# Half-size transfers for the weight chunks of two feed-forward blocks, and another order of PSUM pairs for their last downward product

## The chip, the cores and the metric

The program runs on one core of a Trainium2 chip. The metric is the device time of one execution in microseconds (us), here the median of the runs shown. The engines are TensorE (PE, matrix products; PEld is its loading of weights), VectorE (DVE), ScalarE (ACT), GpSimd (POOL) and SyncE (SP, which here only asks for transfers).

## What is computed

A decoder layer on 1024 tokens of width 1024: a SwiGLU block, a block of three attention branches, a second SwiGLU block. The change touches only the two SwiGLU blocks (d_ff is 2816, 22 tiles of 128):

```python
def _swiglu(h, w_gu, w_down):
    a, b = jnp.split(h @ w_gu, 2, axis=-1)
    return (jax.nn.silu(a) * b) @ w_down

x = x + 0.5 * _swiglu(_rmsnorm(x, ffn1_norm[l]), ffn1_w_gu[l], ffn1_w_down[l])
...
x = x + 0.5 * _swiglu(_rmsnorm(x, ffn2_norm[l]), ffn2_w_gu[l], ffn2_w_down[l])
```

All is float32. The kernel gets that accuracy from a faster format: every operand is split into a high part (`_hi`) and the rest (`_lo`), and each product is three matmuls, hi by hi, hi by lo and lo by hi.

## The kernel before, in words

The instruction streams of the engines are written out by hand, one function per engine; each engine works through its own stream in order, and semaphores tie the streams together. So an instruction that waits holds up all that stands behind it on its engine.

**The feed-forward part.** `ffn(f)` is run twice, f = 0 and f = 1. Its first four tiles are done plainly. The other 18 (`t` = 4 to 21) and the nine pairs of tiles on the way down (`kind` "pair") are done with seven products in place of eight (Strassen's scheme), so sums of blocks of weights are needed. The list `PARTS` is the order: an even tile alone (seven parts), then an odd tile and a pair, whose parts alternate. Two tiles and a pair, 21 parts, are called a triple here; each part is 12 matmuls of 128x512 on PE, so a triple has 252. There are nine triples in each pass. The first pair comes in the first triple, behind the first part of tile 5. Behind the last triple stands the last way down (`kind` "down", four parts, the eight output tiles m = 0 to 7, `down_part`, L2298).

**The weights.** `CHUNK` lists what is loaded: one chunk of 1 MB for each tile and each pair and one for the last way down, 28 in a pass. They alternate between two places, `raw2[0]` and `raw2[1]`, each of two halves of 512 KB. SP asks for chunk c when the last part of chunk c-2 has been split (`chunks`, L718; semaphore `part_split`, counted by DVE). For a pair, c-2 is the even tile of its triple: the pair's chunk is asked for when that tile's last part has been split, and the pair's first part is two places further on in `PARTS`.

**One part's way through the engines.** POOL forms the sums that the part needs (`weights_sum`, L768: S1 and S2, where S2 overwrites one block of the chunk, then S3 and S4). ACT copies to `q_hi` (`part_hi`, L947), DVE subtracts to `q_lo` (`part_lo`, L1526) and counts `part_split`. `q_hi`, `q_lo` and `q_sum` are a ring of four, so a place comes free when PE has done the part four back. For the first part of a pair both S1 and S2 must be there before ACT can copy. DVE works two parts ahead of PE in its stream (`part_lo(f, n + 2)` in `ffn`). Between them stand its other jobs: additions of PSUM results to tiles, the low parts of activations, and `pair_add` (L1523), which adds what a pair's part left in PSUM to `xT`.

**PSUM** is four pairs of banks, `ps[:, 0]` to `ps[:, 3]`. A tile's parts use banks 0 to 3 (pairs 0 and 1); a pair's part uses `ps[:, 2]` for its first six matmuls and `ps[:, 3]` for the others; the last way down also uses `ps[:, 2 + m % 2]`. PE begins a part of a pair, and each output tile m of the last way down, when DVE has taken out what was in that pair of banks (`down_added`).

**Behind the last way down.** In pass 0 DVE and ACT make the operands of the next stage from `xT` while PE works on: `h_hi` (ACT), `h_lo` (DVE, L1387), squares (ACT) summed by POOL (`acc`, then `acc_lo`, L768). PE takes them up in `streamed` and `norm_sum`. In pass 1 PE transposes each finished tile of `xT` (`y_turn`, L2836, into `ps[:, m % 2]`), ACT copies it out and SP stores it.

Of the kernel before, what the change touches and what calls it, by code (L numbers as in the profile page):

```python
# [25 lines left out]
P = 128  # L26
# [122 lines left out]

def add_begin(g):  # L150

    return DT + EVENTS * (g - 1) if g else 0


def chunk_end(c):

    return max(n for n, part in enumerate(PARTS) if part[3] == c) + 1
BR = (HS * HD + 2 * HD + HX * HD) // P
# [164 lines left out]
def layer(nc, x, mem, weights, gains, head_gains, rel_bias, consts, onehot, out):  # L323
    ctx = ExitStack()
    with ctx:
# [172 lines left out]
        raw_in = [sem(f"raw_in{i}") for i in range(NRAW)]  # L498
        hi_done, split_done, unit_done = sem("hi_done"), sem("split_done"), sem("unit_done")
# [201 lines left out]
        def _(sp):  # L701
# [32 lines left out]
            for k in range(U_SB, U_SB + NRAW):  # L734
                if k % NRAW == (CHUNKS - 1) % NRAW:
                    sp.wait_ge(part_split, chunk_end(CHUNKS - NRAW) + 1)
                else:
                    sp.wait_ge(part_split, chunk_end(CHUNKS - NRAW))
                load(k)
# [16 lines left out]
        def _(pool):  # L756
# [13 lines left out]
            def weights_sum(f, n, i, name):  # L770
# [3 lines left out]
                if kind == "tile":  # L774
                    a11, a12, a21, a22 = (raw2[c % 2][:, r, cols] for r in range(2) for cols in BOTH)
# [90 lines left out]
        def _(act):  # L866
# [80 lines left out]
            def part_hi(f, n):  # L947
# [3 lines left out]
                after_chunk(act, f, c)  # L951
# [21 lines left out]
                elif p == 2:  # L973
                    act.wait_ge(w_summed, W_SUMS * f + sums_through(n))
                    src = raw2[c % 2][:, 1, T0]
                else:
                    src = raw2[c % 2][:, p // 6, 512 * (p > 0):512 * (p > 0) + 512]
# [394 lines left out]
        def _(dve):  # L1372
# [79 lines left out]
            def add_tile(f, g, m):  # L1452
# [11 lines left out]
                nc.vector.tensor_tensor(xT[:, m, :], xT[:, m, :], ps[:, 2 + m % 2, :], ALU.add).then_inc(down_added, 1)  # L1464
# [60 lines left out]
            def part_lo(f, n):  # L1525
# [27 lines left out]
                elif p == 2:  # L1553
                    src = raw2[c % 2][:, 1, T0]
                else:
                    src = raw2[c % 2][:, p // 6, 512 * (p > 0):512 * (p > 0) + 512]
# [570 lines left out]
        def _(pe):  # L2127
# [115 lines left out]
            def down_mm(m, q, hi, lo, t, first, final, halves=BOTH, within=None):  # L2243

                for cols in halves:
                    if within and cols == T1:
                        within()
                    mm(ps[:, 2 + m % 2, cols], hi, a_hi[t % 4][:, cols], first, False)
                    mm(ps[:, 2 + m % 2, cols], hi, a_lo[t % 4][:, cols], False, False)
                for cols in halves:  # L2250
                    last = mm(ps[:, 2 + m % 2, cols], lo, a_hi[t % 4][:, cols], False, final)
                return last

            def down_plain(f):
# [3 lines left out]
                def whole(m, q):  # L2258
                    return down_mm(m, q, w_hi[:, w_slot(u + 1 + q), m, :], w_lo[:, w_slot(u + 1 + q), m, :], q, q == 0, q == 1)
# [38 lines left out]
            def down_part(f, n, finish):  # L2298
# [4 lines left out]
                def whole(m, q, halves=BOTH, within=None):  # L2303
                    at_ = P * (2 * q + m % 2)
                    return down_mm(m, q, q_hi[n % NQ][:, at_:at_ + P], q_lo[n % NQ][:, at_:at_ + P], 2 * g + q, q == 0, q == 1,
                                   halves, within)
# [75 lines left out]
            def proj(n, hi, lo, there=None, k0=0, k1=DT):  # L2382
# [20 lines left out]
                if n == PR_SB:  # L2403
# [544 lines left out]
```

## Time and profile before

| | us |
|---|---|
| median of 3 runs | 2198.47 |
| lowest and highest | 2197.08, 2198.56 |
| the profiled execution, its own time | 2196.08 |
| its span in the profile | 2194.2 |
| mean granted TensorE clock, of full speed | 0.998 |

PE is busy in 98% of the span. The page of the profile gives busy times, the chain of work that ended last and the costliest groups. For a change of this kind the timeline (instructions in order of time), the waits and the windows (busy time and granted clock in a chosen stretch) are read too. In a row of the timeline the first number is the start, the second the duration, both in us; a bracket at its end gives how long the engine was idle just before, and what it then waited for. Durations of matmuls overlap: two of them in a row start closer together than one lasts.

### The profile page before, as it was taken

What the parts mean: (1) busy time and instruction counts of PE and PEld (TensorE: products, weight loads), DVE (VectorE), ACT (ScalarE), POOL (GpSimd) and SP (SyncE); (2) the same over time, 40 slices, a digit from 0 to 9 for tenths busy, and PEclk for the clock granted to TensorE, in tenths of its full rate; (3) what the DMA queues carried; (4) which work ended last, traced back from release to release, by engine and by line L of the source; (5) the groups of instructions that cost most, each with busy time, mean ns of one, the idle gap of its engine ahead of it and who ended that gap; (6) DMA issues with size and microseconds to landing.
All of it is one profiled execution on the core that took longest, in us unless ns stands there. A gap on an engine that the chain in (4) does not pass through costs nothing.

```text
span 2194.2 us, 26286 instructions
## 1 busy us (share of the span) xinstructions
PE 2160.8 (98%) x9968; PEld 1733.5 (79%) x9968; DVE 1578.4 (72%) x1809; ACT 908.6 (41%) x1433; POOL 453.1 (21%) x396
## 2 busy tenths in 40 slices
PE   8999999999999999999999999999999999999998
PEld 7787888888887777777778888888887888888887
DVE  7878888888888688877535343354877888888885
ACT  6333333333335677846442111233233333344332
POOL 3013322223323122221000000012013322233320
PEclk9999999999999999999999999999999999999999
DMA  5111111111112300011112111131111111111113
GB/s 172 62 50 57 58 58 58 49 35 52 58 58 84 115 20 29 20 48 39 39 21 77 48 58 48 48 125 39 49 49 57 58 58 58 43 37 57 58 58 96
DMA packets 46733, 126.54 MB, mean 58 GB/s; under 512 B 3405, under 2 KB 20077, under 8 KB 46352
## 3 DMA queue, kind: packets, MB, share of 16 engines
q1 hardware_dynamic: 44704, 112.60, 15.5%
q10 hardware_dynamic: 912, 10.11, 1.2%
q0 software_dynamic: 992, 2.15, 0.5%
q8 instruction: 80, 1.31, 0.2%
q14 instruction: 45, 0.37, 0.0%
HBM read 116.42 MB, written 9.87 MB: 58 GB/s over the span
## 4 chain that ended last, share of the span: by engine, by line
PE 78%; DVE 9%; DMA 5%; POOL 4%; issue 3%; ACT 1%; POOLq 0%; DVEq 0%; SPq 0%; ACTq 0%
PE ps L2129 76%; DMA raw<-in_weights 4%; POOL raw L789 2%; POOL q_sum L786 2%; DVE h_lo L1387 1%; DVE q_lo L1557 1%; DVE xT L1523 1%; DVE q_lo L1546 1%; DVE b_sum_lo L1510 1%; DVE a_full L1590 1%; POOL q_sum L792 1%; DVE tok_lo L1439 1%; PE ps L2744 0%; DVE xT L1731 0%; PE ps L2679 0%
## 5 line engine op out<-in xcount | busy, mean ns | idle before, releaser
L2129 PE MATMUL ps<-tok_hi,q_hi 128*128 128x512 f32 x1008 | 392.5, 389 | 0.0
L2129 PE MATMUL ps<-tok_lo,q_hi 128*128 128x512 f32 x1008 | 392.1, 389 | 0.0
L2129 PE MATMUL ps<-tok_hi,q_lo 128*128 128x512 f32 x1008 | 392.1, 389 | 0.0
L2129 PE MATMUL ps<-h_hi,w_hi 128*128 128x512 f32 x960 | 373.1, 399 | 1.7 <-ACT h_hi L1112 1.1
L2129 PE MATMUL ps<-h_lo,w_hi 128*128 128x512 f32 x960 | 363.9, 391 | 0.7 <-DVE h_lo L2041 0.6
L1523 DVE TENSOR_TENSOR xT<-xT,ps 128x1024 f32<-128x1024 f32 x252 | 302.1, 1216 | 33.8 <-PE ps L2129 23.1
L2129 PE MATMUL ps<-h_hi,w_lo 128*128 128x512 f32 x960 | 305.5, 391 | 0.0
L2129 PEld LDWEIGHTS ps<-tok_hi,q_hi 128*128 128x128 f32 x1008 | 189.2, 188 | 40.2 <-issue 1.1
L2129 PEld LDWEIGHTS ps<-h_hi,w_hi 128*128 128x128 f32 x960 | 179.9, 188 | 51.3 <-issue 15.7
L2129 PEld LDWEIGHTS ps<-tok_hi,q_lo 128*128 128x128 f32 x1008 | 189.2, 188 | 39.4
L2129 PEld LDWEIGHTS ps<-tok_lo,q_hi 128*128 128x128 f32 x1008 | 189.2, 188 | 39.1
L2129 PE MATMUL ps<-b_hi,q_hi 128*128 128x512 f32 x504 | 200.9, 399 | 11.0 <-DVE q_lo L1546 5.9
L2129 PEld LDWEIGHTS ps<-h_hi,w_lo 128*128 128x128 f32 x960 | 180.2, 188 | 38.9 <-DVE w_lo L1380 0.5
L2129 PEld LDWEIGHTS ps<-h_lo,w_hi 128*128 128x128 f32 x960 | 180.1, 188 | 36.2 <-DVE h_lo L2041 1.7
L786 POOL TENSOR_TENSOR q_sum<-raw 128x512 f32<-128x512 f32 x72 | 73.1, 1015 | 608.2 <-DMA raw<-in_weights 419.7
L2129 PE MATMUL ps<-b_hi,q_lo 128*128 128x512 f32 x504 | 197.6, 392 | 0.0
L1380 DVE TENSOR_TENSOR w_lo<-raw,w_hi 128x1024 fp32r<-128x1024 f32 x84 | 115.1, 1372 | 76.8 <-ACT w_hi L878 67.4
L2129 PE MATMUL ps<-a_lo,q_hi 128*128 128x512 f32 x352 | 138.6, 394 | 0.0
L765 POOL TENSOR_TENSOR acc<-acc,sq 128x1024 f32<-128x1024 f32 x21 | 53.9, 2564 | 408.0 <-ACT sq L885 407.9
L2129 PEld LDWEIGHTS ps<-b_hi,q_hi 128*128 128x128 f32 x504 | 95.4, 189 | 43.7 <-DVE q_lo L1546 14.3
L1557 DVE TENSOR_TENSOR q_lo<-raw,q_hi 128x512 fp32r<-128x512 f32 x144 | 112.2, 779 | 21.3 <-ACT q_hi L978 21.3
L1981 DVE TENSOR_TENSOR gate<-ps,rB 128x1024 f32<-128x1024 f32 x24 | 29.4, 1224 | 129.9 <-PE ps L2129 129.9
(309 smaller groups left out, 3682.0 us busy)
## 6 DMA issues: line engine op xcount, KB each, us to landing
raw<-in_weights SPq DMA_DIRECT2D x56, 1024.0 KB, 5.0
raw<-in_weights SPq DMA_DIRECT2D x83, 512.0 KB, 3.5
x_keep<-xT ACTq DMA_DIRECT2D x1, 4096.0 KB, 12.4
x_back<-x_keep ACTq DMA_DIRECT2D x1, 4096.0 KB, 12.1
x_nat<-in_x SPq DMA_DIRECT2D x7, 512.0 KB, 7.4
out<-y_nat SPq DMA_DIRECT2D x7, 512.0 KB, 3.2
toe_keep<-toe_row ACTq DMA_DIRECT2D x2, 704.0 KB, 5.8
m_nat<-in_mem SPq DMA_DIRECT2D x1, 1024.0 KB, 8.0
```

Of the source, the lines that this page charges most:

```text
L765: nc.gpsimd.tensor_tensor(acc[:], acc[:], sq[:, k % 2, :], ALU.add).then_inc(acc_done, 1)
L786: nc.gpsimd.tensor_tensor(to, a21, a22, ALU.add).then_inc(w_summed, 1)
L789: nc.gpsimd.tensor_tensor(a21, to, a11, ALU.subtract).then_inc(w_summed, 1)
L792: nc.gpsimd.tensor_tensor(to, a12, a21, ALU.subtract).then_inc(w_summed, 1)
L1380: nc.vector.tensor_tensor(w_lo[:, w_slot(k)].rearrange("p a b -> p (a b)"), raw[:, k % NRAW, :], w_hi[:, w_slot(k)].rearrange("p a b -> p ...
L1387: nc.vector.scalar_tensor_tensor(out=h_lo[:, k, :], in0=xT[:, k, :], scalar=g32[:, gain, k:k + 1], in1=h_hi[:, k, :].bitcast(F32), op0=ALU ...
L1439: nc.vector.tensor_tensor(tok_lo[i][:], tok[i][:], tok_hi[i][:].bitcast(F32), ALU.subtract).then_inc(tok_split, 1)
L1510: nc.vector.tensor_tensor(b_lo(g, i), b_full(g, i), b_hi[i][:].bitcast(F32), ALU.subtract).then_inc(a_ready, 1)
L1523: nc.vector.tensor_tensor(to, to, ps[:, 2 + half, :].rearrange("p (a c) -> p a c", a=2), ALU.add).then_inc(down_added, 1)
L1557: nc.vector.tensor_tensor(q_lo[n % NQ][:], src, hi, ALU.subtract).then_inc(part_split, 1)
L1981: nc.vector.tensor_tensor(gate_tile(m, b), ps[:, merge_pair(m, b), :], rB[:], ALU.mult).then_inc(mg_taken, 1)
L2129: return pe.matmul(o, a, b, start=start, stop=stop, skip_group_check=True)
```

## The change

Three things are done.

1. Each chunk is brought in by two transfers of 512 KB. Each is asked for when its own half of the place is free (`half_end`): for a tile behind parts 4 and 6, for a pair behind parts 3 and 6, for the last way down behind parts 1 and 3. The tile's weights are laid out anew on the host, so that a half is what parts 0 to 4, or 5 and 6, read (S1 of a tile still reads both). POOL and ACT wait for the half or halves that a part reads; the odd places get semaphores of their own (`chunk_in`).
2. The last way down uses other pairs of PSUM: in pass 0 pairs 1, 0, 2, 3, 1, 0, 2, 3 for m = 0 to 7, in pass 1 pairs 1, 0 and then 2, 3 in turn (`end_pair`). m = 0 and 1 so wait for the last tile's readers (`seven_added`, `glu_done`) and not for the last pair's additions. PE's next users of pair 0 wait for the additions (`PR_SB`, `y_turn`).
3. In pass 1 the transposes move to later places: none behind m = 1, two behind m = 5.

```diff
+def end_pair(f, m):
+
+    return (1, 0, 2, 3)[m % 4] if f == 0 or m < 2 else 2 + m % 2
...
+def half_end(c, half):
+
+    kind, of = CHUNK[c]
+    return part_at(kind, of, {"tile": (4, 6), "pair": (3, 6), "down": (1, 3)}[kind][half]) + 1
...
-        def after_chunk(eng, f, c):
-
-            eng.wait_ge(raw_in[c % 2], 16 * ((U_HALVES[f] + 6) // 2 + CHUNKS // 2 * f + c // 2 + 1))
+        def after_chunk(eng, f, c, *halves):
+
+            for half in halves:
+                if c % 2:
+                    eng.wait_ge(chunk_in[half], 16 * (CHUNKS // 2 * f + c // 2 + 1))
+                else:
+                    eng.wait_ge(raw_in[half], 16 * ((U_HALVES[f] + 6) // 2 + CHUNKS // 2 * f + c // 2 + 1))
...
-                    if c == 0:
-                        sp.wait_ge(split_done, U_HALVES[f] + 6)
-                    elif c == 1:
-                        sp.wait_ge(unit_done, U_HALVES[f] + 6)
-                    else:
-                        sp.wait_ge(part_split, NPART * f + chunk_end(c - 2))
-                    sp.dma_start(raw2[c % 2][:], weights[chunk_at(f, c):chunk_at(f, c) + 2].rearrange("a p n -> p a n")
-                                 ).then_inc(raw_in[c % 2], 16)
+                    for half in range(2):
+                        if c == 0:
+                            sp.wait_ge(split_done, U_HALVES[f] + 6)
+                        elif c == 1:
+                            sp.wait_ge(unit_done, U_HALVES[f] + 6)
+                        else:
+                            sp.wait_ge(part_split, NPART * f + half_end(c - 2, half))
+                        sp.dma_start(raw2[c % 2][:, half, :], weights[chunk_at(f, c) + half]
+                                     ).then_inc((raw_in, chunk_in)[c % 2][half], 16)
...
                 if i == 0:
                     after_slot(pool, f, n)
-                    after_chunk(pool, f, c)
+                    after_chunk(pool, f, c, *((0, 1) if kind == "tile" else (0,) if p < 4 else (1,)))
...
-                after_chunk(act, f, c)
+                if kind == "tile":
+                    after_chunk(act, f, c, 0 if p < 5 else 1)
+                elif kind == "pair":
+                    after_chunk(act, f, c, *((0,) if p < 3 else (0, 1) if p == 3 else (1,)))
+                else:
+                    after_chunk(act, f, c, p // 2)
...
-                    for m in range(2):
-                        pe.wait_ge(down_added, G + m - 1)
-                        whole(m, 0)
+                    pe.wait_ge(seven_added, 3 * TILES7 * (f + 1))
+                    whole(0, 0)
+                    pe.wait_ge(glu_done, (TILE_COUNT - 2) * (f + 1))
+                    whole(1, 0)
                 pe.wait_ge(a_ready, A_COUNT * (f + 1))
                 for m in (2 * p, 2 * p + 1):
                     if p:
-                        pe.wait_ge(down_added, G + m - 1)
+                        pe.wait_ge(down_added, G + m - (1 if f or p == 1 else 3))
...
                 if n == PR_SB:
+                    pe.wait_ge(down_added, ADD_COUNT - 2)
...
+                if m == 0:
+                    pe.wait_ge(down_added, 2 * ADD_COUNT - DT + 2)
...
-            ffn(1, lambda m: y_turn(m - 1) if m else None)
+            def y_behind(m):
+
+                for k in ((), (), (0,), (1,), (2,), (3, 4), (5,), (6,))[m]:
+                    y_turn(k)
+
+            ffn(1, y_behind)
```

The order of instructions, SP, the transfers of pass 0 and the one behind them. `raw_0` and `raw_1` are the two places of chunks. Before:

```order
L727 DMA raw_0_121<-in_weights 128x2x1024 [waits split_done]
L727 DMA raw_1_122<-in_weights 128x2x1024 [waits unit_done]
L727 DMA raw_0_121<-in_weights 128x2x1024 [waits part_split]
L727 DMA raw_1_122<-in_weights 128x2x1024 [waits part_split]
...
L716 DMA raw<-in_weights 128x1024 [waits part_split] x2
```

The same place of SP's stream now:

```order
L748 DMA raw_0_121<-in_weights 128x1024 [waits split_done] x2
L748 DMA raw_1_122<-in_weights 128x1024 [waits unit_done] x2
L748 DMA raw_0_121<-in_weights 128x1024 [waits part_split] x2
L748 DMA raw_1_122<-in_weights 128x1024 [waits part_split] x2
...
L736 DMA raw<-in_weights 128x1024 [waits part_split] x2
```

Each chunk has become two transfers with a wait each, in the same sequence; nothing else on SP moved.

PE, pass 1, where the last pair's part ends and the last way down begins (`a_hi_81` and `a_hi_82` are the last two activation tiles, `cst,xT` a transpose). Before:

```order
L2129 MATMUL ps<-b_hi_90,q_lo_127 128x512
L2129 MATMUL ps<-a_hi_81,q_hi_124 128x512 [waits down_added,a_ready,part_split]
...
L2129 MATMUL ps<-a_hi_81,q_hi_124 128x512 [waits down_added]
...
L2129 MATMUL ps<-a_hi_82,q_hi_124 128x512 [waits a_ready]
...
L2129 MATMUL ps<-a_hi_82,q_lo_128 128x512 x2
L2836 MATMUL ps<-cst,xT 128x128 [waits down_added,glu_done]
L2836 MATMUL ps<-cst,xT 128x128 x7
L2129 MATMUL ps<-a_hi_81,q_hi_125 128x512 [waits down_added,a_ready,part_split]
```

Now:

```order
L2153 MATMUL ps<-b_hi_90,q_lo_127 128x512
L2153 MATMUL ps<-a_hi_81,q_hi_124 128x512 [waits seven_added,a_ready,part_split]
...
L2153 MATMUL ps<-a_hi_81,q_hi_124 128x512 [waits glu_done]
...
L2153 MATMUL ps<-a_hi_82,q_hi_124 128x512 [waits a_ready]
...
L2153 MATMUL ps<-a_hi_82,q_lo_128 128x512 x2
L2153 MATMUL ps<-a_hi_81,q_hi_125 128x512 [waits down_added,a_ready,part_split]
...
L2865 MATMUL ps<-cst,xT 128x128 [waits down_added,glu_done]
```

The first two waits for `down_added` became waits for a tile's readers, and the first transpose moved behind m = 2.

## Rows read from the trace of the kernel before

**Rows 1.** Page, part 1: busy us, share of span, instructions of each engine.
```profile
PE 2160.8 (98%) x9968; PEld 1733.5 (79%) x9968; DVE 1578.4 (72%) x1809; ACT 908.6 (41%) x1433; POOL 453.1 (21%) x396
```
**Rows 2.** Chain that ended last, two pieces of it: start us, us, what.
```profile
162.82 4.92 DMA raw<-in_weights
...
237.54 41.06 PE ps L2129 x180
```
**Rows 3.** Timeline, third triple of pass 0: start us, us, engine, line, operation.
```profile
275.02 0.39 PE L2129 MATMUL ps<-tok_hi,q_hi 128*128 128x512 f32 x1
...
279.94 0.37 SPq L727 DMA_DIRECT2D raw<-in_weights  x1
...
284.95 0.73 POOL L786 TENSOR_TENSOR q_sum<-raw 128x256 f32<-128x256 f32 x1 [12.82 <-DMA raw<-in_weights]
...
286.58 0.39 PE L2129 MATMUL ps<-tok_hi,q_hi 128*128 128x512 f32 x1
...
286.62 0.42 ACT L967 ACTIVATE q_hi<-raw 128x256 fp32r<-128x256 f32 x1 [5.54 <-POOL raw L789]
...
287.96 1.51 DVE L1546 TENSOR_TENSOR q_lo<-q_sum,q_hi 128x256 fp32r<-128x256 f32 x1
...
289.53 0.50 PE L2129 MATMUL ps<-b_hi,q_hi 128*128 128x512 f32 x1
...
294.18 2.34 DVE L1523 TENSOR_TENSOR xT<-xT,ps 128x1024 f32<-128x1024 f32 x2
...
295.53 0.47 PE L2129 MATMUL ps<-b_hi,q_hi 128*128 128x512 f32 x1 [0.23 <-DVE xT L1523]
```
**Rows 4.** Waits of PE, then of PEld, 160 to 676 us: us in total, times, longest.
```profile
PE ps L2129 <- DVE xT L1523: 2.1, 8, 0.3
...
PEld ps L2129 <- DVE q_lo L1546: 7.0, 9, 3.0
```
**Rows 5.** Transfers, whole span: count, KB each, median us from issue to landing.
```profile
raw<-in_weights SPq DMA_DIRECT2D x56, 1024.0 KB, 5.0
raw<-in_weights SPq DMA_DIRECT2D x83, 512.0 KB, 3.5
```
**Rows 6.** Timeline, first pair of pass 0.
```profile
155.57 0.69 DVE L1557 TENSOR_TENSOR q_lo<-q_sum,q_hi 128x512 fp32r<-128x512 f32 x1
...
172.40 0.50 PE L2129 MATMUL ps<-b_hi,q_hi 128*128 128x512 f32 x1 [2.62 <-DVE q_lo L1546]
```
**Rows 7.** Windows, PE alone: us, busy (matmuls), clock, DMA: two stretches behind stops.
```profile
172.40:176.80 4.40, 4.40 (x12) 0.61 0.00 0
...
2158.60:2163.10 4.50, 4.47 (x13) 0.62 0.00 0
```
**Rows 8.** Timeline, last way down of pass 1.
```profile
2157.27 2.34 DVE L1523 TENSOR_TENSOR xT<-xT,ps 128x1024 f32<-128x1024 f32 x2
...
2158.63 0.47 PE L2129 MATMUL ps<-a_hi,q_hi 128*128 128x512 f32 x1 [2.61 <-DVE xT L1523]
...
2163.04 0.40 PE L2129 MATMUL ps<-a_hi,q_hi 128*128 128x512 f32 x1
```
**Rows 9.** Timeline, last way down of pass 0 and what follows.
```profile
676.49 0.47 PE L2129 MATMUL ps<-a_hi,q_hi 128*128 128x512 f32 x1 [2.67 <-DVE xT L1523]
...
680.89 2.58 DVE L1464 TENSOR_TENSOR xT<-xT,ps 128x1024 f32<-128x1024 f32 x2 [2.81 <-PE ps L2129]
...
697.80 0.50 PE L2129 MATMUL ps<-a_hi,q_hi 128*128 128x512 f32 x1 [0.38 <-DVE xT L1464]
...
704.49 6.84 DVE L1387 SCALAR_TENSOR_TENSOR h_lo<-xT,g,h_hi 128x1024 fp32r<-128x1024 f32 x3
...
711.42 3.31 POOL L768 TENSOR_TENSOR acc_lo<-acc,acc_hi 128x1024 fp32r<-128x1024 f32 x1 [1.17 <-ACT acc_hi L890]
```
**Rows 10.** Timeline, an even tile's second part on DVE.
```profile
267.42 0.69 DVE L1557 TENSOR_TENSOR q_lo<-q_sum,q_hi 128x512 fp32r<-128x512 f32 x1 [0.66 <-POOL raw L789]
```
**Rows 11.** Windows, three triples (295.53 to 469.60 us): us, then busy us, summed, then the mean.
```profile
sum 174.07, PE 172.99 PEld 141.47 DVE 143.52 ACT 67.29 POOL 51.68; mean PE 57.66 PEld 47.16 DVE 47.84 ACT 22.43 POOL 17.23
```

More of the change, by code:

```diff
@@ L498, in layer @@
         raw_in = [sem(f"raw_in{i}") for i in range(NRAW)]
+        chunk_in = [sem(f"chunk_in{i}") for i in range(2)]
         hi_done, split_done, unit_done = sem("hi_done"), sem("split_done"), sem("unit_done")
@@ L734, in _ @@
             for k in range(U_SB, U_SB + NRAW):
[L735 to L738, printed above, removed]
+                sp.wait_ge(part_split, half_end(CHUNKS - NRAW, k % NRAW))
                 load(k)
@@ L774, in weights_sum @@
                 if kind == "tile":
-                    a11, a12, a21, a22 = (raw2[c % 2][:, r, cols] for r in range(2) for cols in BOTH)
+                    a11, a21, a12, a22 = (raw2[c % 2][:, r, cols] for r in range(2) for cols in BOTH)
                     to = slot[:]
@@ L1463, in add_tile @@
                     dve.wait_ge(part_done, NPART * f + part_at("down", g, m // 2) + 1)
-                nc.vector.tensor_tensor(xT[:, m, :], xT[:, m, :], ps[:, 2 + m % 2, :], ALU.add).then_inc(down_added, 1)
+                pair = end_pair(f, m) if g else 2 + m % 2
+                nc.vector.tensor_tensor(xT[:, m, :], xT[:, m, :], ps[:, pair, :], ALU.add).then_inc(down_added, 1)
             def add_end():
@@ L1553, in part_lo @@
                 elif p == 2:
-                    src = raw2[c % 2][:, 1, T0]
+                    src = raw2[c % 2][:, 0, T1]
                 else:
-                    src = raw2[c % 2][:, p // 6, 512 * (p > 0):512 * (p > 0) + 512]
+                    src = raw2[c % 2][:, p // 5, BOTH[p // 6]]
                 nc.vector.tensor_tensor(q_lo[n % NQ][:], src, hi, ALU.subtract).then_inc(part_split, 1)
@@ L2241, in seventh, with down_mm @@
                 last.then_inc(part_done, 1)
-            def down_mm(m, q, hi, lo, t, first, final, halves=BOTH, within=None):
+            def down_mm(pair, hi, lo, t, first, final, halves=BOTH, within=None):
                 for cols in halves:
@@ L2247, in down_mm @@
                         within()
-                    mm(ps[:, 2 + m % 2, cols], hi, a_hi[t % 4][:, cols], first, False)
-                    mm(ps[:, 2 + m % 2, cols], hi, a_lo[t % 4][:, cols], False, False)
+                    mm(ps[:, pair, cols], hi, a_hi[t % 4][:, cols], first, False)
+                    mm(ps[:, pair, cols], hi, a_lo[t % 4][:, cols], False, False)
                 for cols in halves:
-                    last = mm(ps[:, 2 + m % 2, cols], lo, a_hi[t % 4][:, cols], False, final)
+                    last = mm(ps[:, pair, cols], lo, a_hi[t % 4][:, cols], False, final)
                 return last
@@ L2304, in whole @@
                     at_ = P * (2 * q + m % 2)
-                    return down_mm(m, q, q_hi[n % NQ][:, at_:at_ + P], q_lo[n % NQ][:, at_:at_ + P], 2 * g + q, q == 0, q == 1,
+                    return down_mm(end_pair(f, m), q_hi[n % NQ][:, at_:at_ + P], q_lo[n % NQ][:, at_:at_ + P], 2 * g + q, q == 0, q == 1,
                                    halves, within)
@@ L2892, in down, with seven @@
         return [w_down[f * P:(f + 1) * P] for f in range(GT * g, GT * g + GT)]
+    def seven(t):
+        gate, up = tile(t)
+        return [np.concatenate([w[:, half * 512:half * 512 + 512] for w in (gate, up)], axis=1) for half in range(2)]
     def pair(g):
@@ L2899, in swiglu_units @@
     plain = tile(0) + tile(1) + tile(2)[:1] + down(0) + tile(2)[1:] + tile(3)
-    chunks = [unit for kind, of in CHUNK for unit in (tile(of) if kind == "tile" else pair(of))]
+    chunks = [unit for kind, of in CHUNK for unit in (seven(of) if kind == "tile" else pair(of))]
     return plain, chunks
```

6 lines of the change are left out of this document (3 added, 3 removed).

## The prediction, made before the changed kernel had run

> **What bounds the kernel now.** Read the busy times first: PE works in 98% of the span, so only 33.4 us (2194.2 less 2160.8) are idle in all, and whatever the change does, it can pay only there and where matmuls run at half clock [rows 1]. Then read the chain of waits: it runs through PE, except that once in a triple it goes through a weight transfer of 4.9 us, and behind it through POOL, ACT and DVE, before it comes back to PE [rows 2] for a stretch such as the 180 matmuls from 237.54. Then the timeline at such a place, to see how long PE stands. Its beat without stops is 0.2267 us a matmul: 51 of them between 275.02 and 286.58 [rows 3]. The chunk for the pair is asked for at 279.94, POOL begins at 284.95 after 12.82 idle, ACT has waited 5.54 for it, the last piece of `q_lo` is ready at 289.47, and PE starts the pair's first part at 289.53. By its beat it would have started at 286.58 + 2.72 = 289.30. So a chain of 9.5 us ends only 0.2 us too late. DVE then has a queue, its two additions begin at 294.18, and PE stops again before the pair's second part, for the first addition, until 295.53 [rows 3]. Both stops come back: eight waits for `xT`, nine of the weight loading for that `q_lo` [rows 4]. The ninth is the first pair's, where the same chain is longer than its cover: PE idle for 2.62 us [rows 6]. The last waits to be seen are at the last way down, 2.67 and 2.61 us for an addition [rows 8, 9].
>
> **Part 1, the half transfers: the pairs of triples 2 to 9.** The price of both stops together is read from a triple's length. Three triples take 174.07 us, one 58.02 [rows 11]; 252 matmuls at 0.2267 are 57.13; the stops cost 0.89. Eight such triples in each pass make 16 x 0.89 = 14.3 us. After the change the pair's first half is asked for behind part 4 of the even tile, two parts or 5.4 us earlier than behind part 6, and a transfer of 512 KB lands in 3.5 us where 1 MB took 5.0 [rows 5]. So the data are there 6.9 us earlier. Then the ring is late next, not the transfer: POOL must wait until PE has left the place four parts back, near 281.1 on the old clock (two parts before 286.58), where it began at 284.95. That is 3.8 us earlier, and `q_lo` is held further by DVE's order only until about 285.5, well before 289.3. DVE, which idled while it waited for this chunk, does its queue in that time; the addition that begins at 294.18 then begins when PE has done the pair's first half, near 290.9, and ends at 292.1 with PE wanting it at 295.0. Both stops go. I take all 14.3; if only the first stop goes and DVE's queue stays as late, the second (bracket 0.23, and 0.16 since a matmul lasts 0.39 against a beat of 0.23) and its slow restart of some 0.1 remain, 16 x 0.5 = 8 us, so the lower end of the gain is 6.3.
>
> **The first pair of each pass.** Its stop costs 2.62 + 0.16 = 2.78, and behind it twelve matmuls took 4.40 us instead of 2.72, at a granted clock of 0.61, which is 1.2 GHz for most of them: 1.68 more [rows 6, 7]. Together 4.46, twice (pass 1 has the same stop, one of the same size): 8.9 us. The transfer was asked for at 162.82 [rows 2]; part 4 had been split at 155.57 + 0.69 = 156.3 [rows 6]. So the first half lands near 159.8 instead of 167.7 (162.82 + 4.92). POOL then starts by the ring, when PE has left the fifth part, near 161.3 (169.6 less three parts of 2.72 and the drain). From the landing to PE's start it took 4.7 us before; I allow 6, since DVE now has other work at that moment: 167.4, before PE wants it at 169.6 (172.40 - 2.78). What is late next is nothing on PE. Bounds 0 and 8.9; I take 8.9, since 2.2 us of slack are left.
>
> **What the halves add.** SP issues 56 more transfers, at 0.37 us each [rows 3], on a queue that otherwise waits: nothing. The second half must not come late: POOL's S1 of a tile reads both. It is asked for when the whole was asked for before (behind part 6), alone in the queue, so by its row it lands at 3.5 instead of 5.0. For the even tile's second part `q_lo` was ready at 268.1 [rows 10] while PE wanted it at 289.30 less seven parts of 2.72, 270.26: 2.1 us of slack. The extra waits of ACT and POOL lie under that. The Trainium skill, "DMA: Bandwidth & Descriptors", section "Bandwidth", speaks against such a split: transfers should be batched to 1 MiB or more to come near the peak rate. By that rule the pair of halves would take longer than the whole, and the traffic would grow; the rows agree (3.5 twice against 5.0), yet no stage here is bound by the rate, so the sum stays.
>
> **Part 2, the last way down, pass 1.** PE waited 2.61 + 0.16 = 2.77 us for DVE's additions of the last pair, which stand in DVE's stream behind low parts for the last way down [rows 8]. The new pairs were read last by the last tile's additions, which are done before. From 2158.63 to 2163.04 the first twelve matmuls took 4.41 instead of 2.72, at a clock of 0.62: 1.69 more [rows 7, 8]. Together 4.46. What is late next is m = 2, which waits for the addition of m = 0: its results are out when PE has 1.36 us left before m = 2 and DVE needs 1.2 and the signal, so 0.2 us are lost, as the first transpose lost before at this place. The eight transposes are only moved; the last ones stand where they stood: nothing.
>
> **Part 2, pass 0.** The same stop is 2.67 + 0.16 = 2.83 us long, and three smaller ones follow, the last of them and the largest 0.38 + 0.16 = 0.54 [rows 9]. But here DVE is the bound. It stands idle 2.81 us until PE has finished m = 0 at 680.89, and from there it works without a pause to 711.33 on additions and `h_lo` [rows 9]; PE waits for the last `h_lo`, and for POOL's `acc_lo`, which ends at 714.73. Only the shift of DVE's start counts: 2.8 us. What PE gains beyond that, up to 1.6, and some 0.7 that it stood there already, it spends waiting for `h_lo`: about 2.3 us. The new wait ahead of `PR_SB` is for the addition of m = 5, due by then. Bounds 0 and 4.4 (2.83 and at most 3 x 0.54); I take 2.8, where DVE's queue puts it.
>
> **The sum.** 14.3 + 8.9 + 4.5 + 2.8 = 30.5 us. The profiled execution took 2196.08, of which 2194.2 are its span and 1.9 lie around it: 2196.1 - 30.5 = 2165.6. It lay 2.4 us below the median of the runs, so the median should be 2198.5 - 30.5 = 2168.0.
>
> **Rivals.**
> 1. *Half clock at a new stop.* In pass 0 PE now stands some 2.3 us before `norm_sum`; stops of 2.6 us were followed by twelve matmuls mostly at 1.2 GHz in both stretches of rows 7, but not at 676.49, where m = 0, eighteen matmuls on, was complete by 680.89, which is their 4.08 us at the full beat and the drain [rows 9]. If the clock falls here, 1.7 us and the delay of `norm_sum` come back, about 2.6: 2170.6.
> 2. *The small stops stay in part.* If DVE's queue, not the transfer, delays the second stop: 8 us less gained, 2176.0. For it: DVE is busy 47.8 of 58.0 us in each triple [rows 11]. Against it: that queue formed behind the late chunk, and 10.2 us of idle time are there to work it off.
> 3. *The chunks do not move the first pair.* If the ring or the low parts of activations hold the first pair as long, 8.9 us stay: 2176.9. Against it are the 2.2 us of slack worked out above.
> 4. *No change.* If PE's stops all move to a next wait of the same length: 2196 to 2200. The slacks worked out above, 2 us and more at each place but the 0.2 at m = 2, speak against it.
> 5. *Slower: POOL stretches DVE.* A DVE subtraction of 256 columns took 1.51 us beside POOL's work, one of 512 columns without it 0.69 [rows 3, 10]. POOL's sums now start while DVE is in the thick of its queue. The point from which it decides is DVE's idle 10.2 us in a triple (58.0 - 47.8); if all of POOL's 17.2 us came on top of DVE's 47.8, a triple would be 65.0, or 7.0 longer, 16 x 7.0 = 112 us: 2310. The gain is eaten once DVE's work grows by more than 12.1 us a triple (10.2, and 30.5 / 16 = 1.9). Against it: much of the overlap is in the 47.8 already. The Trainium skill, "SBUF — State Buffer", section "SBUF: two separate sides", says that one port pair is held by either DVE with two SBUF inputs or GpSimd for a whole instruction. By that rule each meeting costs DVE at most one POOL instruction; the trace agrees, 1.51 being less than 0.69 and one POOL instruction of 1.3.
>
> **How the numbers follow.** All parts as summed: 0.62. Rival 1: 0.12. Rivals 2 and 3 together: 0.19. No change: 0.04. Slower: 0.03. The median of a measurement of this kernel can tell 0.2%, 4.4 us, from no change. Faster by more: 0.93; within: 0.04; slower: 0.03. The likeliest is 2168.0. The range takes in both clock cases and rivals 2 and 3 and stops before no change; below it leaves 3 us for a pass-0 gain of 4.4 and the runs' spread: 2165 to 2178.
>
> **What would show it.** In the new profile the triple from pair to pair should be 57.1 to 57.2 us, PEld's waits for the pair's `q_lo` should be gone from both passes, and the windows at the first pairs should show a clock of 1.00. PE's first matmul of the last way down should follow the pair's last by one beat. In pass 0 DVE's 2.81 us of idle ahead of the addition of m = 0 should be nearly gone. What would make it wrong: a triple still at 57.5 or more, with PE waiting for `xT`; POOL starting late because the ring holds it; or a stop at `h_lo` with a clock of 0.6 behind it.

## The result and the profile after

The changed kernel takes **2167.64 us** (median, 2167.03 to 2168.46); the kernel before took 2197.77 us beside it (2195.73 to 2198.56). The ratio is 0.9865, with a 95% interval of 0.9847 to 0.9882. That is 30.1 us less; the two profiled spans differ by 29.1 us (2194.2 and 2165.1). The forecast was 2168.0 us, 30.5 less.

First part 1 of the page after, its chain by engine, two of its groups (shape | busy us, mean ns | idle us before them, and what ended it) and its transfers of weights (count, KB each, median us from issue to landing). They answer to [rows 1, 2, 5].

```profile
PE 2146.0 (99%) x9968; PEld 1733.8 (80%) x9968; DVE 1584.1 (73%) x1809; ACT 911.7 (42%) x1433; POOL 468.8 (22%) x396
...
PE 92%; DVE 5%; issue 1%; ACT 1%; DMA 0%; POOL 0%; SPq 0%; DVEq 0%; ACTq 0%
...
L2153 PE MATMUL ps<-h_lo,w_hi 128*128 128x512 f32 x960 | 363.9, 391 | 2.6 <-DVE h_lo L1410 2.1
...
L804 POOL TENSOR_TENSOR q_sum<-raw 128x512 f32<-128x512 f32 x72 | 78.7, 1093 | 526.9 <-PE ps L2153 366.6
...
raw<-in_weights SPq DMA_DIRECT2D x195, 512.0 KB, 3.6
```

Three things are to be seen. PE's idle time fell from 33.4 to 19.1 us (2165.1 less 2146.0), which is only half of the gain; the other half lay in "busy" time: in matmuls at half clock, and in those on both sides of each stop, whose records last 0.39 to 0.50 us where the beat is 0.23. The transfer is gone from the chain, which is now 92% PE. And POOL's sums of weights, which [rows 3] showed waiting for `raw`, now wait mostly for PE: 366.6 of the 526.9 us. For the pairs the ring of four places sets their start, as forecast; the sums of each even tile, which read both halves, still wait for the transfer (eight waits in pass 0, 10.3 us at most), at no cost to PE.

The chain of waits that ended last (start, us, what) shows the same as single pieces. Between the first pair and the last way down of each pass it left PE once in a triple, for a transfer and what hung on it [rows 2]; now it is one piece of 2208 matmuls in each pass:

```profile
167.90 500.77 PE ps L2153 x2208
668.72 3.02 PE ps L2153 x12
...
694.40 3.39 DVE h_lo L1410
697.84 23.92 PE ps L2153 x102
...
1636.02 500.78 PE ps L2153 x2208
2136.85 3.01 PE ps L2153 x12
```

Windows over the second and third triple of pass 0 after (us, busy us and count of each engine, granted clock, share of the DMA engines, GB/s) answer to [rows 11]; 58.02 us have become 57.10 and 57.20:

```profile
229.90:287.00 57.10, 57.10 (x253) 47.31 (x252) 47.66 (x60) 22.59 (x42) 17.96 (x16) 1.00 0.18 56
287.00:344.20 57.20, 57.20 (x254) 47.36 (x253) 47.91 (x61) 22.59 (x42) 17.70 (x16) 1.00 0.17 56
```

The third triple's timeline after, for [rows 3] (start, us, engine, line, operation, idle time and what ended it):

```profile
277.07 0.74 POOL L804 TENSOR_TENSOR q_sum<-raw 128x256 f32<-128x256 f32 x1 [9.08 <-PE ps L2153]
...
281.62 1.52 DVE L1570 TENSOR_TENSOR q_lo<-q_sum,q_hi 128x256 fp32r<-128x256 f32 x1
...
284.99 0.39 PE L2153 MATMUL ps<-b_hi,q_hi 128*128 128x512 f32 x1
...
287.31 1.21 DVE L1547 TENSOR_TENSOR xT<-xT,ps 128x1024 f32<-128x1024 f32 x1
```

The pair now begins at 284.99, 4.54 us earlier than 289.53, so POOL's 277.07 is 281.6 on the old clock; the forecast said 281.1. The pair's last `q_lo` is ready at 283.14, 1.85 us before PE wants it, and the first addition, now at 287.31, is made in time.

The first triple of each pass has **two new stops** that the forecast did not have. PE, DVE and POOL at the first of these places after:

```profile
161.59 0.74 POOL L804 TENSOR_TENSOR q_sum<-raw 128x256 f32<-128x256 f32 x1 [9.42 <-PE ps L2153]
...
162.41 1.07 POOL L807 TENSOR_TENSOR raw<-q_sum,raw 128x256 f32<-128x256 f32 x1
162.81 1.23 DVE L1534 TENSOR_TENSOR a_lo<-a_full,b_hi 128x512 fp32r<-128x512 f32 x1
...
163.96 0.68 DVE L1605 TENSOR_TENSOR a_up_half<-a_up_half,ps 128x512 f32<-128x512 f32 x1
...
164.73 0.47 PE L2153 MATMUL ps<-tok_hi,q_hi 128*128 128x512 f32 x1 [0.50 <-issue]
164.74 1.41 DVE L1608 SCALAR_TENSOR_TENSOR a_full<-a_up_half,a_full 128x512 f32<-128x512 f32 x1
...
165.67 1.62 POOL L807 TENSOR_TENSOR raw<-q_sum,raw 128x512 f32<-128x512 f32 x1
166.07 1.77 DVE L1581 TENSOR_TENSOR q_lo<-raw,q_hi 128x512 fp32r<-128x512 f32 x1
...
167.90 0.50 PE L2153 MATMUL ps<-tok_hi,q_hi 128*128 128x512 f32 x1 [0.18 <-DVE q_lo L1581]
```

The `q_lo` of 512 columns takes 1.77 us, and PE takes it up at once. In the kernel before, the same operation took 0.68, while POOL stood idle (DVE's timeline before):

```profile
164.70 0.68 DVE L1557 TENSOR_TENSOR q_lo<-raw,q_hi 128x512 fp32r<-128x512 f32 x1
```

By PE's beat of 0.227 us the two stops cost 0.66 and 0.34 us; with the slow matmuls right behind them it is 1.1 us a pass. Pass 1 has the same two at 1632.86 and 1636.02. The pair itself, which in [rows 6] waited 2.62 us, follows without a stop.

At the last way down of pass 0, for [rows 9] (the first row is the last pair's last matmul):

```profile
662.84 0.39 PE L2153 MATMUL ps<-b_hi,q_lo 128*128 128x512 f32 x1
663.07 0.39 PE L2153 MATMUL ps<-a_hi,q_hi 128*128 128x512 f32 x1
...
667.35 1.22 DVE L1488 TENSOR_TENSOR xT<-xT,ps 128x1024 f32<-128x1024 f32 x1 [1.29 <-PE ps L2153]
...
697.84 0.50 PE L2153 MATMUL ps<-h_lo,w_hi 128*128 128x512 f32 x1 [2.10 <-DVE h_lo L1410]
```

The stop of 2.67 us and the three small ones are gone: PE begins at 663.07, one beat behind the pair. It stands before the last `h_lo` instead, 2.10 + 0.16 us. DVE's addition of m = 0 has moved from 680.89 to 667.35, 13.54 us; that is what pass 0 gives. Its idle time before it fell from 2.81 to 1.29 us, and not to nearly nothing.

### The profile page after: what moved, and what is told of

Same layout as the page of the kernel before. It is cut to its first block, busy times and chain, and to the rows that moved or that the text cites. A ratio compares the mean times of both kernels' runs of the same rounds, so it can differ in the third digit from the quotient of the medians.

```text
span 2165.1 us, 26379 instructions
## 1 busy us (share of the span) xinstructions
PE 2146.0 (99%) x9968; PEld 1733.8 (80%) x9968; DVE 1584.1 (73%) x1809; ACT 911.7 (42%) x1433; POOL 468.8 (22%) x396
## 2 busy tenths in 40 slices
DMA packets 47630, 126.55 MB, mean 58 GB/s; under 512 B 4301, under 2 KB 20973, under 8 KB 47248
## 4 chain that ended last, share of the span: by engine, by line
PE 92%; DVE 5%; issue 1%; ACT 1%; DMA 0%; POOL 0%; SPq 0%; DVEq 0%; ACTq 0%
PE ps L2153 91%; DVE h_lo L1410 1%; DVE tok_lo L1462 1%; PE ps L2770 0%; DVE xT L1755 0%; DVE q_lo L1581 0%; PE ps L2705 0%; DVE h_lo L2065 0%; DVE xT L1488 0%; PE ps L2865 0%; DVE w_lo L1403 0%; DMA x_nat<-in_x 0%; ACT sb_l L1212 0%; POOL sb_l L829 0%; DVE a_lo L1534 0%
## 5 line engine op out<-in xcount | busy, mean ns | idle before, releaser
L2153 PE MATMUL ps<-b_hi,q_hi 128*128 128x512 f32 x504 | 196.1, 389 | 0.0
L804 POOL TENSOR_TENSOR q_sum<-raw 128x512 f32<-128x512 f32 x72 | 78.7, 1093 | 526.9 <-PE ps L2153 366.6
L1001 ACT ACTIVATE q_hi<-q_sum 128x512 fp32r<-128x512 f32 x108 | 68.3, 632 | 142.0 <-POOL q_sum L810 58.2
L1581 DVE TENSOR_TENSOR q_lo<-raw,q_hi 128x512 fp32r<-128x512 f32 x144 | 124.0, 861 | 0.0
```

The lines of the kernel that those rows point to most:

```text
L804: nc.gpsimd.tensor_tensor(to, a21, a22, ALU.add).then_inc(w_summed, 1)
L1001: nc.scalar.activation(q_hi[n % NQ][:], src, ACT.Copy).then_inc(part_hi_done, 1)
L1581: nc.vector.tensor_tensor(q_lo[n % NQ][:], src, hi, ALU.subtract).then_inc(part_split, 1)
L2153: return pe.matmul(o, a, b, start=start, stop=stop, skip_group_check=True)
```

## The experiments

All medians have the kernel before beside them on the same chip. The first 43 us of a kernel hang on when `x` arrives (PE waits for `x_nat`), and differ from profile to profile by 1.1 us. So I also give the span less the start of the first matmul on `m`, the one of this row in the changed kernel:

```profile
43.12 0.68 PE L2153 MATMUL ps<-mT_hi,w_hi 128*128 128x256 f32 x1
```

Where it says "matmul by matmul", each matmul's start, counted from that one, is compared with the start of the same matmul in the other kernel's trace. Two profiles of the changed kernel itself end 0.1 us apart by this count.

| kernel | median us | before, same chip | span less start on `m` |
|---|---|---|---|
| before | 2197.77 | | 2151.1 |
| changed | 2167.64 | 2197.77 | 2122.0 |
| halves_only | 2170.39 | 2197.22 | 2125.0 |
| psum_only | 2188.10 | 2197.22 | 2144.0 |
| late_halves | 2169.16 | 2197.22 | 2125.5 |
| pool_later | 2167.49 | 2197.22 | 2122.9 |
| pass0_old | 2168.11 | 2196.82 | 2123.6 |
| pass0_short | 2166.61 | 2196.82 | 2122.2 |
| turns_old | 2168.16 | 2196.82 | 2124.7 |
| pool_fourth | 2167.26 | 2196.82 | 2122.2 |
| pool_tile | 2166.71 | 2195.92 | 2122.6 |
| pool_two | 2165.59 | 2195.92 | 2120.9 |
| changed, again | 2166.52 | 2195.92 | 2122.1 |

### Each part alone

**halves_only**, the changed kernel without the banks' new order, its waits and the new places of the transposes (the first of the diff's lines):

```
-    return (1, 0, 2, 3)[m % 4] if f == 0 or m < 2 else 2 + m % 2
+    return 2 + m % 2
...
-                    pe.wait_ge(seven_added, 3 * TILES7 * (f + 1))
-                    whole(0, 0)
-                    pe.wait_ge(glu_done, (TILE_COUNT - 2) * (f + 1))
-                    whole(1, 0)
+                    for m in range(2):
+                        pe.wait_ge(down_added, G + m - 1)
+                        whole(m, 0)
...
```

> The changed kernel with the banks, waits and transposes of the kernel before: of the change only the transfers in halves are left. If the prediction's sum holds, the pass ends lose again what the banks' order had won, 4.46 us at the last way down of pass 1 and 2.8 us in pass 0: 2167.6 + 7.3 = 2174.9 us. A rival in which the halves did all the work and the banks' order none gives 2167.6 us. A rival in which the two parts overlap, so that a stop comes back shorter, lies between.

Measured: 2170.39 us, 2.8 above the changed kernel and not 7.3. The stops at both last ways down came back, but at half their size, and the twelve matmuls behind the one in pass 1 ran at full clock. PE at both places, the window behind the second (us, busy, clock, DMA, GB/s), and DVE's addition of m = 0 in pass 0:

```profile
664.77 0.47 PE L2153 MATMUL ps<-a_hi,q_hi 128*128 128x512 f32 x1 [1.24 <-DVE xT L1547]
...
669.17 1.22 DVE L1488 TENSOR_TENSOR xT<-xT,ps 128x1024 f32<-128x1024 f32 x1 [2.82 <-PE ps L2153]
...
2134.43 0.47 PE L2153 MATMUL ps<-a_hi,q_hi 128*128 128x512 f32 x1 [1.24 <-DVE xT L1547]
...
2134.43:2138.84 4.41, 4.41 (x19) 1.00 0.01 4
```

**psum_only**, the kernel before with the banks' order, its waits and the moved transposes, and whole transfers:

```
+def end_pair(f, m):
+
+    return (1, 0, 2, 3)[m % 4] if f == 0 or m < 2 else 2 + m % 2
...
-                    for m in range(2):
-                        pe.wait_ge(down_added, G + m - 1)
-                        whole(m, 0)
+                    pe.wait_ge(seven_added, 3 * TILES7 * (f + 1))
+                    whole(0, 0)
+                    pe.wait_ge(glu_done, (TILE_COUNT - 2) * (f + 1))
+                    whole(1, 0)
...
```

> The kernel before with the banks' order, its waits and the place of the transposes alone; weights still come in one transfer of a whole chunk. The prediction's sum gives 2197.8 - 4.46 - 2.8 = 2190.5 us. A rival in which the banks' order is worth nothing by itself gives 2197.8 us. If the two parts add without overlap, what this run gains and what halves_only gains add up to the 30.1 us of the whole change.

Measured: 2188.10 us, 9.1 below before; by the last column 7.1. Matmul by matmul the two last ways down by themselves give 3.0 and 4.4 us, so alone the banks are worth what the sum gave them. (The column's 7.1 also holds one half clock at a first pair, where before's profile has two, and slightly longer small stops.) But alone the two parts give 26.8 and 9.1 us, 35.9 together, and both at once 30.1: they share the stops at the passes' ends. With one transfer in halves the last pair's additions come earlier, which leaves a stop of 1.40 us of 2.78 and no half clock; the banks then take away that rest. In pass 1 the halves have 2.77 + 1.69 - 1.40 = 3.06 of the 4.46 and the banks 1.40; in pass 0 the banks' share is DVE's idle time, 2.82 less 1.29, 1.5 us. Together 2.9, as measured. The traces so explain 4.5 of the 5.8 us (3.06 and, in pass 0, 2.83 less 1.40) of overlap. By the table's last column the overlap is smaller too, 26.1 + 7.1 - 29.1 = 4.1 us; the rest of the 5.8 lies within the spread of the times of before (2195.7 to 2198.6).

### What in the halves does it

**late_halves** asks for both halves where before the whole chunk was asked for:

```
-    return part_at(kind, of, {"tile": (4, 6), "pair": (3, 6), "down": (1, 3)}[kind][half]) + 1
+    return part_at(kind, of, {"tile": (6, 6), "pair": (6, 6), "down": (3, 3)}[kind][half]) + 1
```

> The changed kernel, with both halves of a chunk asked for together, behind the last part of the chunk that had the place, where the kernel before asks. It separates asking earlier from moving less per transfer. Theory (the earlier request does the work): the first pairs' stops come back in part, 1.4 us each and up to 1.7 us of half clock each, 2.8 to 6.2 us in all, and 0 to 3 us of the small stops in the steady triples: 2171 to 2177 us. Rival (the first half of a chunk is there in 3.5 us and not in 5.0, which alone does it): 2167.6 us.

Measured: 2169.16 us, 1.5 above the changed kernel (3.5 from the start on `m`, of which 1.4 is half clock at a place that the edit does not touch): below the theory's 2171 and above the rival's 2167.6. POOL's first sum and the pair's start in the first triple, then the window over a later triple:

```profile
166.05 0.73 POOL L804 TENSOR_TENSOR q_sum<-raw 128x256 f32<-128x256 f32 x1 [14.35 <-DMA raw<-in_weights]
...
170.59 0.50 PE L2153 MATMUL ps<-b_hi,q_hi 128*128 128x512 f32 x1 [1.28 <-DVE q_lo L1570]
...
234.60:291.70 57.10, 57.10 (x254) 1.00 0.15 56
```

The stop of the first pair is 1.28 us, half of the 2.62 of [rows 6], as the theory said, with no half clock behind it. But in triples 2 to 9 the shorter transfer alone removes everything: 57.10 us. The 14.3 us of the sum's largest term need only the 1.4 us by which 512 KB lands sooner than 1 MB (the chain was 0.2 us too long). Asking earlier brings POOL from 166.05 to 161.59 and is worth only what is left at the first pairs: matmul by matmul 1.0 us in pass 0 and 0.9 in pass 1, about 2 in all (1.5 by the medians), since it also makes the two new stops.

### The passes' ends

**pass0_old**, the changed kernel with pass 0's last way down in the pairs and behind the waits of before (pass 1 new):

```
-    return (1, 0, 2, 3)[m % 4] if f == 0 or m < 2 else 2 + m % 2
+    return (1, 0)[m] if f and m < 2 else 2 + m % 2
...
```

> The changed kernel with the last way down of pass 0 in the banks and behind the waits of the kernel before; pass 1 keeps the new order. By the prediction's term for pass 0 this costs 2.8 us: 2167.6 + 2.8 = 2170.4 us. By the trace of halves_only, where TensorE's first stop there is 1.24 us and no longer 2.67 (the chunk in halves brings the pair's additions forward), it costs the 1.5 us by which that trace falls behind the changed kernel's over this stretch: 2169.1 us. If pass 0 is bound by DVE in such a way that the order does not matter: 2167.6 us.

Measured: 2168.11 us; from the start on `m` 1.6 longer than the changed kernel. The second figure, 1.5, is right and the prediction's 2.8 is not what this part is worth inside the whole.

**pass0_short**, pass 0's last way down ordered like pass 1's, each product waiting for one addition and not for three:

```
-    return (1, 0, 2, 3)[m % 4] if f == 0 or m < 2 else 2 + m % 2
+    return (1, 0)[m] if m < 2 else 2 + m % 2
...
-                        pe.wait_ge(down_added, G + m - (1 if f or p == 1 else 3))
+                        pe.wait_ge(down_added, G + m - 1)
```

> The changed kernel with the last way down of pass 0 in the order of pass 1: pairs 1, 0 and then 2 and 3 in turn, each with the wait of one addition and not of three. The prediction calls this stretch bound by DVE's additions and by its low parts of the gate. By that, TensorE's stops of 0.2 to 0.4 us between the additions come back and its stop before the gate's projection, 2.26 us in the changed kernel, shrinks by as much: 2167.6 us, within 0.3. The rival, in which TensorE and not DVE is the bound of the stretch, loses the small stops, some 1.2 us: 2168.8 us.

Measured: 2166.61 us; from the start on `m` 2122.2, 0.2 from the changed kernel (the lower median is matched by 2166.52 in the changed kernel's second run). PE's waits from 600 to 710 us, first in pass0_short, then in the changed kernel (us in total, times, longest):

```profile
PE ps L2153 <- DVE xT L1488: 1.1, 3, 0.4
...
PE ps L2153 <- DVE h_lo L1410: 2.1, 1, 2.1
```

Three small stops came back and the wait for `h_lo` went below the view's bound, for nothing either way. DVE is the bound here, as the prediction said; the four pairs of banks that pass 0 uses in turn bring nothing beyond the first two.

**turns_old**, the output's transposes one tile earlier, where they were:

```
-                for k in ((), (), (0,), (1,), (2,), (3, 4), (5,), (6,))[m]:
+                for k in ((), (0,), (1,), (2,), (3,), (4,), (5,), (6,))[m]:
```

> The changed kernel with the output's transposes at the places of the kernel before, each one tile earlier, in the last way down of pass 1. The prediction gave moving them nothing: 2167.6 us. The rival: with the first additions only now made beside the way down, the first transpose waits in TensorE's order for the sum of its tile, and TensorE stands for 1.3 to 1.5 us: 2168.9 to 2169.1 us. A stop of over 2 us could also be followed by half clock, up to 1.7 us more.

Measured: 2168.16 us; from the start on `m` 2.7 longer, of which 1.4 lie behind a half clock in pass 0 that has nothing to do with the edit (below), so 1.3. The rival is right. The stop is this one:

```profile
2139.12 0.33 PE L2865 MATMUL ps<-cst,xT 128*128 128x128 f32 x1 [1.31 <-DVE xT L1488]
```

With the new pairs nothing was added to m = 0 earlier, so the first transposes must stand back for that sum. Moving them was no gain by itself, but without it the banks' order would have given its 1.4 us in pass 1 away again.

### The two new stops

**pool_later** holds POOL's sums for the first pair, and so all behind them, until the eight parts ahead are split:

```
+                    if PARTS[n][:3] == ("pair", 1, 0):
+                        pool.wait_ge(part_split, NPART * f + n)
```

> The changed kernel, in which the sums that POOL makes for the first pair of each pass wait until the eight parts of the tiles ahead of it are split. In the changed kernel the first triple of each pass has two new stops of TensorE, 1.19 us a pass; the DVE operations ahead of them took 1.23 to 1.77 us where 0.68 us was usual, beside sums of POOL. If POOL beside DVE is the cause, the two stops go and nothing takes their place: 2167.6 - 2.4 = 2165.2 us. If the cause is another (the halves' landing, or ACT), the stops stay: 2167.6 us. If the sums now come too late for the pair, its stop comes back, with up to 1.7 us of half clock: 2168 to 2172 us.

Measured: 2167.49 us, no gain (0.9 us longer from the start on `m`). The cause is right: without POOL beside it, DVE's operations took 0.68 us again and both stops went. The third outcome came true as well, smaller: the pair was late.

```profile
164.56 0.69 DVE L1583 TENSOR_TENSOR q_lo<-raw,q_hi 128x512 fp32r<-128x512 f32 x1
...
170.28 0.50 PE L2155 MATMUL ps<-b_hi,q_hi 128*128 128x512 f32 x1 [0.64 <-DVE q_lo L1572]
...
176.30 0.47 PE L2155 MATMUL ps<-b_hi,q_hi 128*128 128x512 f32 x1 [0.26 <-DVE xT L1549]
```

**pool_fourth** was to hold back only the sums at 164.31 and 165.67 us; the diff is that of pool_tile with `("pair", 1, 1)`.

> The changed kernel, in which POOL's first two sums for the first pair of each pass keep their time and only the third and fourth wait for the low part of the tile's last part. Holding all of them back (pool_later) took away TensorE's two stops in the tile, 0.66 and 0.34 us, and gave 0.79 and 0.42 us at the pair instead. Theory (POOL beside DVE, by place): the second stop goes, the first stays, and the pair is in time: 0.3 to 0.4 us less a pass, 2166.8 to 2167.1 us. Rival: the pair's low part comes late here too and gives the same 2167.5 us.

Measured: 2167.26 us, both stops unchanged (0.66 and 0.36 us). The theory was not tested: parts of tile and pair alternate in POOL's order, and those two sums are the odd tile's second part, not the pair's. What the run does show is that the sums behind them, held back by some 2 us, do no harm or good.

**pool_tile** and **pool_two** put that right; pool_tile, and for pool_two the condition that replaces its first line:

```
+                    if PARTS[n][:3] == ("tile", 5, 1):
+                        pool.wait_ge(part_split, NPART * f + n - 1)
...
+                    if PARTS[n][:3] in (("pair", 1, 0), ("tile", 5, 1)):
```

> The changed kernel, in which POOL holds back only the two sums that stood beside the stretched operation of DVE: those of the odd tile's second part in the first triple of each pass (164.31 and 165.67 us in the changed kernel), until the low part of that tile's first part is done. pool_fourth had held back sums that come later and changed nothing. Theory (POOL beside DVE): that low part takes 0.68 us and not 1.77, TensorE's second stop, 0.34 us, goes and the first, 0.66, stays: 0.3 us less a pass, 2167.0 us. Rival (another cause): both stops stay, 2167.6 us.

> As pool_tile, and POOL also waits with the first two sums for the pair until the last part of the even tile is split, which is 1 us later. Theory: the first stop, 0.66 us, shrinks as well, since DVE's reading of TensorE's banks is no longer behind a stretched operation; the pair's low part still comes before TensorE wants it: up to 1.0 us less a pass, 2165.6 us. Rival: the pair comes late, as in pool_later, where the two stops in the tile went and two others of 1.2 us in all took their place: 2167.5 us.

Measured: 2166.71 and 2165.59 us. DVE and POOL in pool_tile:

```profile
165.03 0.69 DVE L1583 TENSOR_TENSOR q_lo<-raw,q_hi 128x512 fp32r<-128x512 f32 x1
165.63 0.68 DVE L1536 TENSOR_TENSOR b_sum_lo<-b_sum,b_hi 128x512 fp32r<-128x512 f32 x1
165.85 1.62 POOL L806 TENSOR_TENSOR q_sum<-raw 128x512 f32<-128x512 f32 x1 [2.68 <-DVE q_lo L1583]
166.24 0.68 DVE L1613 TENSOR_TENSOR a_full<-a_full,ps 128x512 f32<-128x512 f32 x1
```

The `q_lo` takes 0.69 us and not 1.77, and the second stop is gone; POOL's sum now takes the longer time. At the `h_lo` stop of pass 0 pool_tile is 0.4 us ahead of the changed kernel, counted from the start on `m`. In pool_two the first stop goes too, and one of 0.42 us comes at the pair's second part, for an addition. In all it is 1.1 us ahead, and 0.9 by the medians on one chip; pool_tile is 0.8 ahead once the 1.4 us of half clock that its profile shows are taken off. So the second edit is mostly traded away, and the first is worth about 0.4 us a pass. pool_two at 2165.59 us has the lowest median of this study, though its single executions overlap with those of the changed kernel beside it (2165.34 to 2166.95 against 2166.47 to 2167.03).

**after_again** is the changed kernel itself.

> The changed kernel once more, unchanged, on the same chip as the two runs above, to see what comes back and what does not: 2167.6 us. The 2.10 us stop ahead of the projection with the low part of the gate was followed by a granted clock of 1.00 in the first profile, but a stop of the same length at the same place was followed by 0.64 to 0.67 in late_halves and turns_old. If this hangs on the edits, it is 1.00 here again; if it is a matter of the single execution, it can be either, and the time of an execution is then 1.6 us longer.

Measured: 2166.52 us and a clock of 1.00 behind the same stop. The median is 1.1 lower than on the first chip, and before was 1.9 lower beside it: differences of a microsecond need the traces, or one chip.

## Why the prediction was right, and where not

**Triples 2 to 9, 14.3 us: right.** 58.02 became 57.10 to 57.20, and no stop is left. The mechanism was given too much, though: late_halves shows that the shorter transfer suffices and that the 5.4 us of earlier asking were not needed.

**First pairs, 8.9 us: the stop was right, its neighbourhood was not.** The stop and its half clock went in both passes. The step that failed is "I allow 6" and "what is late next is nothing on PE": the pair's `q_lo` ended at 169.71 and not at 167.4, 8.1 us behind POOL's start at 161.59 and not 6 (the wanted start, 169.6, had itself moved with the new stops to 170.75), so the slack was 1.0 us and not 2.2, and POOL's earlier sums pushed PE's tile by 1.0 to 1.1 us a pass. Rival 5 named this mechanism, POOL beside DVE, but looked for it in the steady triples, where it costs nothing, and priced it only as a disaster or nothing. The net term is 8.9 - 2.2 = 6.7.

**What the halves add: nothing, as forecast.** By the rule that the forecast cites, the traffic would have grown. It did not: the page has 126.54 MB before and 126.55 after, in 46733 and 47630 packets, and each half landed in 3.6 us.

**Last way down, pass 1, 4.46 us, and pass 0, 2.8 us: right as sums, wrong as the banks' own.** In the prediction each part's gain was read from the trace of before alone. psum_only confirms them there. In the changed kernel 3.06 and 1.4 us of them come from the halves already. The total holds, since the stop could only go once. The same oversight made "DVE's idle time nearly gone" wrong: it is 1.29 us, because DVE's queue is now that much ahead of PE. The 0.2 us lost at m = 2 is there in both passes (0.21 by PE's beat); in pass 0 the kernel before had it at m = 2 too.

**"The eight transposes are only moved: nothing"** is true of the cost and hid a condition: leaving them would have cost 1.3 us.

**The sum.** 30.5 foreseen, less 2.2 for the new stops, is 28.3; the spans differ by 29.1 and the medians by 30.1. Matmul by matmul the terms came out as 9.0 for the first pairs (8.9 foreseen), 14.8 for the triples (14.3), 3.0 for the last way down of pass 0 (2.8) and 4.4 for that of pass 1 (4.5), less 2.2 for the new stops: 29.0. The time of 2168.0 came out 0.4 us too high because before's median was 0.7 us lower in this comparison (2197.77 and not 2198.47) and the gain 0.4 us smaller. At that size agreement is luck as much as working.

**Rival 1, half clock at the new stop in pass 0,** is not in the first profile but in three of nine, see below: 0.12 was too low for a single execution, and the 2.6 us too much, for the three lost 1.4 each.

## What to carry to other kernels

Here a chain through a transfer ended 0.2 us too late 16 times, and a shorter first transfer was enough. Read how much is lacking before adding an earlier request, because the work that starts earlier lands beside other work. When two changes aim at the same stop, price the second in a kernel that has the first. A stop on PE can be paid for by an engine that runs early: look for operations that grew (0.68 to 1.77 us), and hold back just the one beside them.

## What the runs showed of the hardware

**The same stop is followed by half clock in some executions and not in others.** PE's stop for `h_lo` in pass 0 lasted 2.09 to 2.14 us in all nine profiles that have it. In six (changed, changed again, psum_only, pool_later, pool_fourth, pool_two) the matmuls behind it kept their beat; in three they did not. The stop and its window in late_halves, the window in pool_tile, and the changed kernel's:

```profile
698.44 0.50 PE L2153 MATMUL ps<-h_lo,w_hi 128*128 128x512 f32 x1 [2.11 <-DVE h_lo L1410]
...
698.44:702.60 4.16, 4.16 (x12) 0.64 0.89 378
...
697.09:701.30 4.21, 4.21 (x11) 0.59 0.88 374
...
697.84:702.10 4.26, 4.26 (x18) 1.00 0.87 369
```

turns_old has 0.67 there. A granted clock of 0.59 to 0.67 is 1.2 GHz for most of those matmuls. The matmuls behind them come 1.4 us later in each of the three, counted matmul by matmul. In psum_only the first pairs show it within one execution: the same stop of 2.61 us in pass 0 and 2.62 in pass 1, and behind them

```profile
171.72:176.10 4.38, 4.38 (x19) 1.00 0.01 2
1650.13:1654.60 4.47, 4.47 (x13) 0.64 0.00 0
```

The mean granted clocks of all executions, profiled or not, point the same way: psum_only's four have 0.999, 0.998, 1.000 and 1.000 (2188.36, 2189.43, 2187.85 and 2187.07 us), and the changed kernel's eight have 0.999 twice (2168.46 and 2167.79 us). These means do not tell the place, and pass0_old's profile has 0.999 with no half clock behind any stop, so they only support it.

So a stop of 2.1 to 2.8 us costs its length and, sometimes, 1.4 to 1.7 us more; the six stops of 1.2 to 1.3 us (halves_only, late_halves, pass0_old, turns_old) were followed by full clock each time. What decides between the two is open. The Trainium skill, "TensorE: Matmul & The Clock Gate", Part 1, says that the gate watches activity on a clock of its own that a kernel's start does not reset; with that, stops of one length could fall either way, as here, but no run here tests it.

**POOL and DVE side by side.** A DVE subtraction of two SBUF tensors took 0.68 us alone and 1.23 to 1.77 beside a sum of POOL, while one that reads a bank of PSUM (`a_full<-a_full,ps` in pool_tile) kept 0.68. In the first triple of the changed kernel the subtractions of 1.23 and 1.77 us end 0.56 and 0.55 us behind the end of the sum that they met: 164.04 against POOL's 163.48, and 167.84 against 167.29. They look as if they had stood until POOL was done. The Trainium skill, "SBUF — State Buffer", section "SBUF: two separate sides", has the reason as a port pair that either POOL or a DVE instruction with two SBUF inputs holds for a whole instruction; the trace agrees in both cases.
